# A transformer block in fp32: gate and up panels as seven quarter products of pairs, with the down projection moved behind them

## The reference, cut to what matters

```python
def swiglu(h, w_gu, w_down):
    g, u = jnp.split(h @ w_gu, 2, axis=-1)
    return (jax.nn.silu(g) * u) @ w_down
# ...
hf = rmsnorm(x, norm_ffn_g[l])
x = x + swiglu(hf, w_gu[l], w_down[l])
return rmsnorm(x, final_norm_g)
```

## Time and profile before

| | us |
|---|---|
| median of 3 runs | 2831.89 |
| lowest, highest | 2831.8, 2834.16 |
| the profiled execution, its own time | 2832.06 |
| its span, first to last instruction | 2830.3 |

### The profile page before, as it was taken

One profiled execution on the slowest core, in us unless ns is written; L12 is line 12 of the kernel. 1 busy time (PEld: TensorE's weight loads), 2 busy tenths in 40 slices (PEclk: granted clock), 3 DMA queues, 4 the chain that ended last, 5 costly groups with the idle time before them and its releaser, 6 DMA issues.

```text
span 2830.3 us, 34874 instructions
## 1 busy us (share of the span) xinstructions
PE 2795.2 (99%) x13038; PEld 2320.2 (82%) x13038; DVE 1341.8 (47%) x1534; ACT 895.1 (32%) x1150; POOL 99.7 (4%) x98
## 2 busy tenths in 40 slices
PE   9999999999999999999999999999999999999997
PEld 7888888888788888896788888888888888888886
DVE  6667733345633354664644434343444444343435
ACT  6545432225632232343422222222222222222224
POOL 0000000000000003500200000000000000000000
PEclk9999999999999999999999999999999999999999
DMA  6222233232223252241222222222222222222222
GB/s 239 67 89 74 67 101 102 91 103 77 68 97 101 92 191 92 96 146 60 93 97 97 97 96 96 96 96 96 96 96 96 96 96 96 96 96 96 97 96 82
DMA packets 79179, 280.10 MB, mean 99 GB/s; under 512 B 8720, under 2 KB 12816, under 8 KB 78480
## 3 DMA queue, kind: packets, MB, share of 16 engines
q1 hardware_dynamic: 78688, 278.95, 29.4%
q10 hardware_dynamic: 432, 0.32, 0.0%
HBM read 275.05 MB, written 4.19 MB: 99 GB/s over the span
## 4 chain that ended last, share of the span: by engine, by line
PE 95%; DVE 2%; ACT 1%; DMA 1%; issue 0%; SPq 0%; DVEq 0%; ACTq 0%
PE acc L1437 25%; PE acc L1438 25%; PE acc L1439 25%; PE acc L1462 5%; PE acc L1463 5%; PE acc L1464 5%; DMA x_tokens<-x_n 1%; PE ps L1504 1%; PE ps L1493 1%; DVE w_lo L841 1%; ACT w_hi L440 0%; PE ps L1517 0%; PE ps L1518 0%; PE ps L1516 0%; ACT ps L630 0%
## 5 line engine op out<-in xcount | busy, mean ns | idle before, releaser
L1437 PE MATMUL acc<-act_hi,w_hi 128*128 128x512 f32 (+1 forms) x2912 | 1126.6, 387 | 1.6 <-DVE sq_sum L1233 1.0
L1439 PE MATMUL acc<-act_hi,w_lo 128*128 128x512 f32 (+1 forms) x2912 | 1120.1, 385 | 0.0
L1438 PE MATMUL acc<-act_lo,w_hi 128*128 128x512 f32 (+1 forms) x2912 | 1119.7, 385 | 0.0
L841 DVE TENSOR_TENSOR w_lo<-raw,w_hi 128x1024 fp32r<-128x1024 f32 x496 | 627.2, 1268 | 521.0 <-ACT w_hi L440 511.2
L440 ACT ACTIVATE w_hi<-raw 128x1024 fp32r<-128x1024 f32 x496 | 522.5, 1056 | 960.3 <-PE acc L1439 620.4
L1437 PEld LDWEIGHTS acc<-act_hi,w_hi 128*128 128x128 f32 x2912 | 547.5, 188 | 111.8 <-issue 1.5
L1439 PEld LDWEIGHTS acc<-act_hi,w_lo 128*128 128x128 f32 x2912 | 547.3, 188 | 109.2
L1438 PEld LDWEIGHTS acc<-act_lo,w_hi 128*128 128x128 f32 x2912 | 547.6, 188 | 107.6 <-issue 1.0
L1462 PE MATMUL acc<-act_hi,w_hi 128*128 128x512 f32 x736 | 288.3, 392 | 2.8 <-DVE x L1196 2.8
L1463 PE MATMUL acc<-act_lo,w_hi 128*128 128x512 f32 x736 | 286.8, 390 | 0.0
L1464 PE MATMUL acc<-act_hi,w_lo 128*128 128x512 f32 x736 | 286.7, 389 | 0.0
(11 more groups left out here) (224 smaller groups left out, 1575.7 us busy)
## 6 DMA issues: line engine op xcount, KB each, us to landing
raw<-w_stream SPq DMA_DIRECT2D x496, 512.0 KB, 3.5
x<-x_t SPq DMA_DIRECT2D x16, 512.0 KB, 8.5
x_tokens<-x_n SPq DMA_DIRECT2D x4, 1024.0 KB, 15.1
out_t<-x SPq DMA_DIRECT2D x7, 512.0 KB, 3.0
mem<-mem_t SPq DMA_DIRECT2D x1, 2048.0 KB, 15.0
out_t<-x SPq DMA_DIRECT2D x2, 256.0 KB, 4.3
qa<-pos ACTq DMA_DIRECT2D x1, 256.0 KB, 2.6
par<-params ACTq DMA_DIRECT2D x1, 60.0 KB, 4.2
```

What stands on the lines that cost most here:

```text
L841: nc.vector.tensor_tensor(w_lo[:, s, :], raw[:, s, :], f(w_hi[:, s, :]), ALU.subtract)\
L1437: nc.tensor.matmul(dst, wh, ah, start=start and k == 0, stop=False)
L1438: nc.tensor.matmul(dst, wh, al, start=False, stop=False)
L1439: last = nc.tensor.matmul(dst, wl, ah, start=False, stop=stop and k == UK - 1)
```

## The change

**Work.** The first DIRECT = 2 hidden tiles are made as before. The other 42 tiles are made in MIXES = 21 pairs. For a pair of tiles the gate (and then the up) is a product of a 2x2 block matrix of weights (two output tiles by two halves of the features) and a 2x2 block matrix of activations (two halves of the features by two halves of the tokens). It is computed with seven products of quarter blocks (Strassen's scheme in Winograd's form) where there were eight.

**Weights.** A mix unit holds four blocks pairs (W21, W11, W12, W22). POOL forms four sums of 128x256 from `raw` (`make_sums`); ACT copies three raw block pairs and the four sums to high parts, DVE makes the low parts. TensorE's unit (`mix_unit`) is seven products of 2 blocks by 3 matmuls of 256 columns, 42 in all; four units make one result of two tiles in four banks. In the first of the four, three of the matmuls are 512 wide: they also write zeros to the other half of their bank.

**Activations.** The sums T1 to T4 are made once: `x` is first written to DRAM, ACT multiplies it by the gain, POOL makes four sums in place (twice, for two parts), ACT and DVE split them to `t_hi` and `t_lo`, which lies where `x` was. `x` is read back from DRAM at the end of the pairs.

**Results.** DVE puts the seven products together (`read_products`), the gate is treated for two tiles at once, and the hidden tiles go to DRAM (`store`, ACT's queue). When all 44 tiles are made, the whole down projection follows: 11 groups of 8 units, whose four hidden tiles are read back and split (`hidden_high`, `hidden_low`) during the group before.

The diff, cut to its core:

```diff
+DIRECT = 2
+MIXES = (FFN // P - DIRECT) // 2
+MIX_UNITS = 8
+MIX_LOOP = 3
+U_MIX = U_FFN + 4 * DIRECT
+U_DOWN = U_MIX + MIX_UNITS * MIXES
+UNITS = U_DOWN + GROUPS * KT // 2
...
+B11, B12, B21, B22 = ((slice(UK * k, UK * (k + 1)), slice(S // 2 * t, S // 2 * (t + 1)))
+                      for k in range(2) for t in range(2))
+T2, T1, T4, T3 = B11, B12, B21, B22
+W11, W12, W22 = range(3)
+S3, S1, S2, S4 = range(4)
+PRODUCTS = (("s", S2, "t", T2, 1, 1), ("w", W12, "b", B21, 1, 0), ("s", S3, "t", T3, 2, 1), ("s", S1, "t", T1, 2, 0),
+            ("w", W22, "t", T4, 3, 1), ("s", S4, "b", B22, 3, 0), ("w", W11, "b", B11, 0, 0))
...
+            t_hi = sb("t_hi", [P, 2 * KT + 1, S // 2], F32R, a)
+            cg = sb("cg", [P, 2, S], F32, a)
+            sgx = sb("sgx", [P, 2, S], F32, a)
+            cu = sb("cu", [P, 2, S], F32, a)
+            wa_hi = sb("wa_hi", [P, 2, 6 * P], F32R, a)
+            wa_lo = sb("wa_lo", [P, 2, 6 * P], F32R, a)
...
+            if n % 3 < 2:
+                return (wa_hi if hi else wa_lo)[:, n % 3, :]
+            return (w_hi if hi else w_lo)[:, RING - 1, 0:6 * P]
+        def sums(hi, n):
+            return (w_hi if hi else w_lo)[:, n % 3, :]
+        def sums_f(n):
+            return (over_hi if n % 2 else over_lo)[:, 0:4, S // 2:S]
+        def bank(n, b):
+            return acc[n][:] if b == 0 else ps[n][:, S * (b - 1):S * b]
...
+            def spill(c):
+                part = slice(X_TILES * c, X_TILES * (c + 1))
+                sp.wait_ge(acc_free, A_XO + X_TILES * (c + 1))
+                sp.dma_start(x_spill[:, part, :], x[:, part, :]).then_inc(x_spilled[c // 2 % 2], 16)
+            for n in range(U_XO, U_MIX):
+                weights(n)
+                if n >= U_XO + 7:
+                    spill(n - U_XO - 7)
+                if n == U_XO + 13:
+                    spill(7)
...
+            for c in range(4):
+                sp.wait_ge(unit_done, U_DOWN - 3 + c)
+                if c < 2:
+                    hidden_in(c)
+                    weights(U_DOWN + 2 + c)
+                x_in_again(c)
+            weights(U_DOWN + 4)
+            for c in range(4, 8):
+                x_in_again(c)
+            weights(U_DOWN + 5)
+            hidden_in(2)
+            hidden_in(3)
...
+            for c in range(2):
+                b11, b12, b21, b22 = (x[:, UK * k + half_k * c:UK * k + half_k * (c + 1), S // 2 * t:S // 2 * (t + 1)]
+                                      for k in range(2) for t in range(2))
+                pool.wait_ge(x_gained, UK * (c + 1))
+                link(nc.gpsimd.tensor_tensor(b22, b12, b22, ALU.subtract))
+                link(nc.gpsimd.tensor_tensor(b12, b12, b11, ALU.subtract))
+                link(nc.gpsimd.tensor_tensor(b11, b11, b22, ALU.subtract))
+                nc.gpsimd.tensor_tensor(b21, b21, b11, ALU.subtract).then_inc(t_made, 1)
+            made = Tally(U_MIX)
+            def make_sums():
+                n = made.n - U_MIX
+                turn = made.n // RING + 1
+                for i, st in made.loops:
+                    turn = i * (st // RING) + turn
+                w21, w11, w12, w22 = (raw[:, n % RING, 2 * P * b:2 * P * (b + 1)] for b in range(4))
+                dst = sums_f(n)
+                pool.wait_ge(raw_in[n % RING], turn * 16)
+                pool.wait_ge(lo_done, made.at(-1))
+                link(nc.gpsimd.tensor_tensor(dst[:, S3, :], w21, w11, ALU.subtract))
+                nc.gpsimd.tensor_tensor(dst[:, S1, :], w21, w22, ALU.add)
+                link(nc.gpsimd.tensor_tensor(dst[:, S2, :], w22, dst[:, S3, :], ALU.add))
+                nc.gpsimd.tensor_tensor(dst[:, S4, :], w12, dst[:, S2, :], ALU.subtract).then_inc(sums_made, 1)
+                made.add()
...
+                    act.wait_ge(raw_in[s], turn * 16)
+                    act.wait_ge(unit_done, converted.at(-2))
+                    nc.scalar.activation(own(True, i), raw[:, s, 2 * P:8 * P], ACT.Copy).then_inc(hi_done, 1)
+                    act.wait_ge(sums_made, mixed.at(1))
+                    nc.scalar.activation(sums(True, i).rearrange("p (a b) -> p a b", a=4), sums_f(i), ACT.Copy)\
+                        .then_inc(sums_hi, 1)
+                    mixed.add()
+                    converted.add()
+            def store(p):
+                act.wait_ge(hid_made, stores.at(1))
+                act.dma_start(hid_t[p, :, :, :], cg[:]).then_inc(hid_stored, 16)
+                stores.add()
...
                     units()
                     std(4, ps[0], rstd, S)
                     units()
                     nc.scalar.preload_act_table_set("sigmoid_and_others")
+                    act.wait_ge(h_lo, 3 * KT)
+                    act.wait_ge(x_spilled[0], 64)
+                    x_gain([*range(4), *range(UK, UK + 4)])
                 else:
+                    units()
+                    mixed_high(0)
+                read_out()
+                nc.scalar.activation(sgx[:, t, :], cg[:, t, :], ACT.Sigmoid).then_inc(sig_ready, 1)
+                if t == 0:
+                    act.wait_ge(x_spilled[1], 64)
+                    x_gain([*range(4, UK), *range(UK + 4, KT)])
                     units(2)
-                read_out()
-                nc.scalar.activation(sg[:], gt[:], ACT.Sigmoid).then_inc(sig_ready, 1)
-                units(2)
-                read_out()
-                nc.scalar.activation(act2_hi[:, t, :], gt[:], ACT.Copy).then_inc(hid_hi, 1)
+                else:
+                    mixed_high(1)
+                    mix_convert(2)
+                out_no.add()
...
+            def pair(p, last=False):
+                mix_convert()
+                act.wait_ge(gated, pair_no.at(1))
+                nc.scalar.activation(sgx[:], cg[:], ACT.Sigmoid).then_inc(sig_ready, 1)
+                mix_convert()
+                if last:
+                    convert(RING - 2)
+                    convert(RING - 2)
+                    hidden_high(0, 32)
+                    convert(RING - 2)
+                else:
+                    mix_convert(4)
+                pair_no.add()
+                store(p)
+                if not last:
+                    mix_convert(2)
...
+                    i, s = converted.n - U_MIX, converted.n % RING
+                    dve.wait_ge(hi_done, converted.at(1))
+                    nc.vector.tensor_tensor(own(False, i), raw[:, s, 2 * P:8 * P], f(own(True, i)), ALU.subtract)
+                    dve.wait_ge(sums_hi, mixed.at(1))
+                    four = "p (a b) -> p a b"
+                    nc.vector.tensor_tensor(sums(False, i).rearrange(four, a=4), sums_f(i),
+                                            f(sums(True, i)).rearrange(four, a=4), ALU.subtract).then_inc(lo_done, 1)
+                    mixed.add()
+                    converted.add()
...
+            def read_products(n, dst):
+                unit.add(4)
+                dve.wait_ge(unit_done, unit.at())
+                out = dst[:].rearrange("p a (h s) -> p (a h) s", h=2)
+                one, two, three, four = (bank(n, b) for b in range(4))
+                halves = "p (a b) -> p a b"
+                link(nc.vector.tensor_copy(out[:, 1, :], one[:, 0:SH]))
+                first = out[:, 1:2, :].broadcast_to([P, 2, SH])
+                link(nc.vector.tensor_tensor(out[:, 0:4:3, :], two.rearrange(halves, a=2), first, ALU.add))
+                u2 = out[:, 3:4, :].broadcast_to([P, 2, SH])
+                link(nc.vector.tensor_tensor(out[:, 1:3, :], three.rearrange(halves, a=2), u2, ALU.add))
+                link(nc.vector.tensor_tensor(out[:, 3, :], three[:, 0:SH], out[:, 2, :], ALU.add))
+                nc.vector.tensor_tensor(out[:, 1:3, :], four.rearrange(halves, a=2), out[:, 1:3, :], ALU.add)                    .then_inc(products_read, 1)
+                group.add()
+                dve.wait_ge(products_read, group.at())
+            both = rstd[:].unsqueeze(1).broadcast_to([P, 2, S])
+            def pair(last=False):
+                dve.wait_ge(hid_stored, stores.at(16))
+                read_products(0, cg)
+                nc.vector.tensor_tensor(cg[:], cg[:], both, ALU.mult).then_inc(gated, 1)
+                mix_low(2)
+                dve.wait_ge(sig_ready, sig.at(1))
+                dve.wait_ge(gated, pair_no.at(1))
+                link(nc.vector.tensor_tensor(cg[:], cg[:], sgx[:], ALU.mult))
+                link(nc.vector.tensor_tensor(cg[:], cg[:], both, ALU.mult))
+                sig.add()
+                if last:
+                    units(2)
+                    hidden_low(0)
+                else:
+                    mix_low(2)
+                read_products(1, cu)
+                nc.vector.tensor_tensor(cg[:], cg[:], cu[:], ALU.mult).then_inc(hid_made, 1)
+                pair_no.add()
+                stores.add(16)
+                if last:
+                    units()
+                else:
+                    mix_low(4)
...
+            def mix_unit(n, c, start):
```

(115 more changed lines are left out.)

255 lines of the change are left out of this document (159 added, 96 removed).

## The result

The changed kernel takes **2813.09 us** (median of four runs, 2810.36 to 2816.80); the kernel before, run beside it, 2831.93. The ratio is 0.9932, 95% interval 0.9915 to 0.9950: faster by 0.7%, 18.8 us. The forecast was 2796, so the sign is right and the time lies in the range, but about half of the 35.8 us forecast is missing. Sums of the trace are made against that.

The account below looks back on a forecast made before the run. TensorE, busy 99% of the span, was taken as the bound. Steady pairs -53.8, into the pairs +14, out +3, loop turns +1 summed to -35.8, from 2831.89 to 2796 us; range 2784 to 2848.

Parts of the forecast that it names:

- The bound, the steady pair: Pairs stage: TensorE bounds it; a result of two tiles takes 20.48 us instead of 21.76, 42 times, -53.8 us.
- Rival (3): 256-wide matmuls are dearer in the pairs than near the kernel's end, or unit starts show: typically 2810 us, chance 0.10.
- plus 1 us for loop turns in all: Pairs stage: unit starts cost TensorE nothing, and all its loop turns together 1 us.
- The upper bound of 20 us: Pairs stage: 168 unit starts at 0.12 us each if every wait shows, kept for the range.
- rivals (2): DVE and POOL mildly bound the pair: TensorE waits 0.2 to 1.7 us per pair, +18, 2814 us, chance 0.15.
- Into the pairs: Start of the pairs: TensorE idles 13 us before the first mix unit, +14 with a unit 1 us late.
- the prediction's rule of mutual exclusion: DVE and POOL hold each other off; queued, a POOL addition costs 0.60 us, a 1024-element DVE low part 1.09.
- Out of the pairs: Turn from pairs to down projection: late hidden tiles, bank read and addition cost +3 us (0 to 8).
- DVE and POOL, "38.8 of 40.96 us": Steady pair: DVE's 19.6 and POOL's 19.2 us of mutually exclusive work fit within TensorE's 40.96, with 2.1 to spare.
- The slack of 2.7 us: Least lead in one followed pair: unit 10 is ready at 28.2 us and wanted at 30.9.
- Rival (4): The transitions into and out of the pairs are twice as long: 2813 us, chance 0.05.
- rival (1): DVE and POOL bound the pair; whole durations exclude each other, 45.7 us a pair, 2896 us, chance 0.17.

Follow-up runs that it names:

- after: The changed kernel itself, measured beside the kernel before: 2813.09 us, ratio 0.9932.
- run 2: After, with ACT making eight gains before the statistic and eight before the first sigmoid, T's first half split ahead of a unit conversion: 2806.57 us.
- run 6: Run 5 plus first unit's sums in `cu`, T's second half split earlier, first two units waiting for four low parts, DVE converting a unit earlier: 2787.17 us.
- run 1: After, with TensorE's program for pairs 4 to 21 written out instead of a loop of six turns: 2807.13 us.
- run 3: After, with the edits of run 1 and run 2 together: 2800.16 us.
- run 5: Run 3 with POOL's sums in four buffers in place of two: 2792.16 us.
- run 4: After, with POOL making the first addition of each mix unit twice, five additions instead of four: 2914.74 us.
- run 9: Run 5 (four sum buffers) with POOL's first addition of each unit made twice: 2907.51 us.
- run 8: The kernel before, with only TensorE's last-stage middle groups changed to three turns of three groups each, all matmuls written out: 2831.53 us.

## Why the prediction was right and wrong

- **The bound, the steady pair: right.** 20.48 us for a result was forecast, 20.50 measured; the earlier trace rows carried over, 0.120 us between 256-wide matmuls, with no bubble at unit starts as the earlier trace rows had it. Rival (3) fell. -53.8 became -52.9.
- **"plus 1 us for loop turns in all": the step that failed.** It measured 16.1 us: five branches of 3.5 to 4.8 us, some half of it covered by the sixteen matmuls that still start, and the lower clock behind them. For the 1 us the prediction gives no row; what it read in the old trace is a unit start and the old turns into the down projection, and neither has a gap. It didn't ask what is new about this loop: a turn of 2016 instructions, longer than any of before, under matmuls half as long. The upper bound of 20 us, kept for another reason (168 unit starts), held the size by accident. That 2813 is what rivals (2) and (4) name is luck as well: in after TensorE loses nothing in the steady pairs to DVE and POOL, and the transitions are not twice as long.
- **Into the pairs: +14, measured +16.1.** The late unit was +1, as said; the gap 14.02 against 13. Missing was the clock: the first result took 21.79 us, +1.3. POOL's eight sums over T ended near the forecast; four low parts of T took DVE 11.75 us beside them, as the prediction's rule of mutual exclusion says. Runs 2 and 6 took 6.5 and 5.0 us of the time away by order, place and a later wait alone; what is left stands where DVE and POOL are both full.
- **Out of the pairs: +3, measured +4.6.** The steps were 0.88 and 2.23 us, for 0.8 and 1.7 forecast; the lower clock behind them is the rest.
- **DVE and POOL, "38.8 of 40.96 us": right for after, but for a wrong reason.** TensorE never waited for them there, yet their round took 41.55 us, more than TensorE's 41.0 and not 2.1 less: the turns' gaps hid that. The slack of 2.7 us was read from one pair, followed from a fresh start; run 1's first six pairs are that, and from the eighth on there was none left. POOL's wait for its two buffers was named and put at nothing, as covered by that slack; in run 3 it is 2 us at every fourth unit, and with four buffers (run 5) the 0.55 us are gone. The chance of 0.17 for the slow end was not idle: one addition more per unit, runs 4 and 9, gives 46.6 us a pair and 2908 to 2915 us, near rival (1)'s 45.7 and 2896. The rule of mutual exclusion that the prediction quotes from the Trainium skill, "SBUF — State Buffer", section "Who interferes with whom", would by whole durations give its 45.7 us. The runs stand between the two sums: at 32 additions a pair fits into 41.0 us, which 45.7 excludes; at 40 an addition costs 1.1 us, which 0.60 doesn't give.
- **Rival (4)**, transitions twice as long: not so; 20.7 us for 17.

## What to carry to other kernels

When a change makes matmuls shorter, look at everything they used to cover: here a branch of 3.6 us is free under sixteen 512-wide matmuls, and branches of 3.3 to 4.8 us cost 1.5 to 3.1 us under sixteen 256-wide ones; keep the turns of TensorE's program short, or write them out. A pipeline of three engines over two buffers can have a round slightly longer than the bound's and show no wait for hundreds of us while the lead lasts: compare late pairs with early ones, and give it buffers before work is taken away. Price a long gap on TensorE with the clock behind it: 1.3, 2.8 and 1.6 us more at three of them in after, and 2.4 in run 1 behind the same gap that cost 1.3.

## What the runs showed of the hardware

- TensorE's branch at the end of a turn: 0.2 us after 1152 instructions, 3.3 to 4.8 after 2016 (after, runs 2 and 4), 3.4 to 3.6 after 3456 (run 8); 15 to 17 matmuls still start meanwhile.
- In after the granted clock fell to 0.50 at the gaps of 14.0, 3.2 and 2.6 us (starts apart) and at one of 2.2 behind one of 0.9, and stayed at 1.00 at three others of 1.9 to 2.2. It came back while matmuls ran, some 3 to 6 us later.
- A 256-column addition on POOL takes 0.73 us alone. Beside a busy DVE its mean is 1.13 us in after (0.92 to 1.46 by group), 1.20 in run 5 and 1.13 with five per unit in run 9, each from 1480 to 2250 us.
